# Two blocks of a transformer on one core: who brings 96 of the 128 rows of the last block of expert weights, and when

## The reference, cut to what matters

```
xe = jax.vmap(lambda hb, ib: hb[ib])(h, idx)
hidden = jax.nn.silu(jnp.einsum('becd,edf->becf', xe, w_gate)) * jnp.einsum('becd,edf->becf', xe, w_up)
ye = jnp.einsum('becf,efd->becd', hidden, w_down) * gate[..., None].astype(h.dtype)
return jax.vmap(lambda ib, yb: jnp.zeros((t, d), yb.dtype).at[ib.reshape(-1)].add(yb.reshape(-1, d)))(idx, ye)
```

## Time and profile before

| | us |
|---|---|
| time, median of 3 runs | 1834.66 (1834.52 to 1834.79) |
| time of the profiled execution | 1835.42 |
| its span | 1833.6 |
| TensorE busy (matmul) | 1443.5, 79% of the span |
| VectorE busy | 689.1, 38% |
| ScalarE busy | 527.5, 29% |
| moved by DMA | 542.02 MB, mean 296 GB/s |

### The profile page before, as it was taken

How to read it: one execution, slowest core, us unless ns; L and a number is a source line. 1 busy time by engine, 2 the same in 40 slices (tenths; PEclk the granted TensorE clock), 3 DMA queues, 4 the chain that set the end, 5 groups by cost and what they waited for, 6 DMA issues and landing times.

```text
span 1833.6 us, 24325 instructions
## 1 busy us (share of the span) xinstructions
PE 1443.5 (79%) x10242; PEld 943.9 (51%) x10251; DVE 689.1 (38%) x1169; ACT 527.5 (29%) x879; POOL 120.2 (7%) x147
## 2 busy tenths in 40 slices
PE   7999999999999999999895565665556655556565
PEld 7887888887888889988642111211111111111121
DVE  5676666666666667887620000000000000000000
ACT  6545443654444576566510000000000000000000
POOL 0151000012000011042200000000000000000000
PEclk9999999999999999999998778878777787887878
DMA  9533555543455644434789999999999999999997
GB/s 274 178 122 129 188 188 184 177 144 116 161 193 193 193 142 139 137 97 184 315 350 426 428 428 427 428 428 426 427 428 428 428 428 427 427 428 428 428 427 324
DMA packets 139283, 542.02 MB, mean 296 GB/s; under 512 B 10173, under 2 KB 103570, under 8 KB 114738
## 3 DMA queue, kind: packets, MB, share of 16 engines
q1 hardware_dynamic: 138968, 540.46, 75.0%
q0 software_dynamic: 48, 0.13, 0.0%
q10 hardware_dynamic: 170, 0.04, 0.0%
HBM read 539.56 MB, written 1.05 MB: 295 GB/s over the span
## 4 chain that ended last, share of the span: by engine, by line
PE 46%; DMA 45%; DVE 4%; ACT 2%; issue 1%; POOL 0%; ACTq 0%; SPq 0%; DVEq 0%; POOLq 0%
DMA ew<-in_expert_w_up_dram 15%; DMA ew<-in_expert_w_gate_dram 15%; DMA ew<-in_expert_w_down_dram 14%; PE bank L1310 8%; PE bank L1617 7%; PE bank L1312 7%; PE bank L1311 7%; PE bank L1615 4%; PE bank L1995 3%; DVE wHL L2056 1%; PE bank L2033 1%; PE bank L1614 1%; PE bank L1533 1%; ACT wHL L825 1%; PE bank L1331 1%
## 5 line engine op out<-in xcount | busy, mean ns | idle before, releaser
L1995 PE MATMUL bank<-ew,xeT 128*32 128x512 f32 x2048 | 342.7, 805 | 233.8 <-DMA ew<-in_expert_w_up_dram 127.7
L2056 DVE TENSOR_TENSOR wHL<-ring,wHL 128x2048 fp32r<-128x2048 f32 (+1 forms) x124 | 284.3, 2294 | 103.3 <-ACT wHL L825 102.6
L1995 PEld LDWEIGHTS bank<-ew,xeT 128*32 128x32 f32 x2048 | 65.0, 129 | 492.3 <-DMA ew<-in_expert_w_up_dram 208.3
L825 ACT ACTIVATE wHL<-ring 128x2048 fp32r<-128x2048 f32 (+1 forms) x124 | 236.6, 1908 | 244.8 <-PE bank L1617 132.2
L2033 PE MATMUL bank<-ew,tok 128*32 128x256 f32 x2048 | 158.6, 464 | 104.8 <-DMA ew<-in_expert_w_down_dram 97.2
L1617 PE MATMUL bank<-xHL,wHL 128*128 128x512 f32 x588 | 210.0, 396 | 0.0
L2761 DVE TENSOR_TENSOR tok<-tok,bank 128x512 f32<-128x512 f32 x16 | 11.0, 688 | 524.7 <-PE bank L1995 524.7
L1615 PE MATMUL bank<-xHL,wHL 128*128 128x256 f32 x672 | 174.1, 279 | 0.0
L2033 PEld LDWEIGHTS bank<-ew,tok 128*32 128x32 f32 x2048 | 71.8, 128 | 186.3 <-DMA ew<-in_expert_w_down_dram 119.5
L2766 DVE TENSOR_TENSOR h<-h,bank 128x512 f32<-128x512 f32 x60 | 37.2, 681 | 293.0 <-PE bank L2041 293.0
L1615 PEld LDWEIGHTS bank<-xHL,wHL 128*128 128x128 f32 x672 | 126.6, 188 | 8.2
(11 more groups left out here) (358 smaller groups left out, 2248.9 us busy)
## 6 DMA issues: line engine op xcount, KB each, us to landing
ew<-in_expert_w_gate_dram SPq DMA_DIRECT2D x64, 2048.0 KB, 46.2
ew<-in_expert_w_up_dram SPq DMA_DIRECT2D x64, 2048.0 KB, 46.0
ew<-in_expert_w_down_dram SPq DMA_DIRECT2D x62, 2048.0 KB, 46.7
ring<-in_w_gate_up_dram SPq DMA_DIRECT2D x44, 1024.0 KB, 5.0
ring<-in_w_down_dram SPq DMA_DIRECT2D x22, 1024.0 KB, 4.9
ring<-in_w_in_dram SPq DMA_DIRECT2D x22, 1024.0 KB, 5.3
ring<-in_w_out_dram SPq DMA_DIRECT2D x12, 1024.0 KB, 4.9
ring<-in_w_in_fox_dram SPq DMA_DIRECT2D x10, 1024.0 KB, 9.4
```

Of the source, the lines that this page charges most:

```text
L825: act.activation(split_part(n, 0, 0, w.stop), ring[:, slot(n), w], ACT.Copy).then_inc(w_hi, 1)
L1995: mm = pe.matmul(bank[half][32 * j:32 * j + 32, :], xeT[:, k, CAP * e:CAP * e + CAP], w_[:, m, 512 * j:512 * j + 512], start=(k == 0), sto ...
L2056: op = dve.tensor_tensor(split_part(n, 1, c0, c1 - c0), ring[:, slot(n), c0:c1], split_part(n, 0, c0, c1 - c0).bitcast(F32), ALU.subtract)
```

## The change

SP's three parts of the last unit hold only rows (partitions) 96 to 127: 32 rows instead of 128. Rows 0 to 95 are issued by ScalarE, whole rows of 16 KB, in twelve transfers of 8 rows. ScalarE issues them ahead of its work for the last expert, when unit 181 has been used, the same condition as SP's for its parts. They count on a semaphore of their own (`e_near`), 16 for each, and TensorE waits for all twelve before the first matmul of the last unit. The bytes moved and all the arithmetic stay as they are.

```diff
@@
+        NEAR, NEAR_ROWS = 96, 8
...
-        e_end = x_in[0]
+        e_end, e_near = x_in[0], x_in[1]
...
-                    sp.dma_start(ew[:, eslot(g), c], src[:, c]).then_inc((e_full[eslot(g)], e_rest, e_end)[part], 16)
+                    sp.dma_start(ew[NEAR:P, eslot(g), c], src[NEAR:P, c])\
+                        .then_inc((e_full[eslot(g)], e_rest, e_end)[part], 16)
...
             for e in range(NE):
+                if e == NE - 1:
+                    act.wait_ge(e_used, LAST - ESLOTS + 1)
+                    near = e_down[0, e].rearrange("(u p m) d -> u p (m d)", p=P, m=4)[EU - 9]
+                    for r in range(0, NEAR, NEAR_ROWS):
+                        act.dma_start(ew[r:r + NEAR_ROWS, eslot(LAST), :], near[r:r + NEAR_ROWS, :]).then_inc(e_near, 16)
                 act.wait_ge(e_used, e * EU + 4)
...
                 for j in range(4):
+                    if e * EU + 8 + j == LAST:
+                        pe.wait_ge(e_near, 16 + 16 * (NEAR // NEAR_ROWS))
                     w_ = arrived(8 + j).rearrange("p (m d) -> p m d", m=4)
```

## The result

The changed kernel takes 1861.12 us (median of 6 runs, 1858.04 to 1866.78), the kernel before 1834.59 (6 runs, 1834.14 to 1835.40): a ratio of 1.015 with a 95% interval of 1.0139 to 1.0160, 26.5 us slower. Forecast were 1833.1 us and a range of 1832.4 to 1840.6. The profiled execution has a span of 1859.5 us (time 1861.33).

A forecast was written before the change was run, and what follows sets the result against it. The experts' stage was taken as bound by the DMA weight stream at 428 GB/s. Last bytes 3.5 us sooner, less lost cover of small parts, gave -1.6 us from 1834.66: 1833.1 us, range 1832.4 to 1840.6.

The forecast's parts named there:

- a transfer of 8 rows runs on eight engines: ScalarE's twelve transfers: one row per engine, always the same eight engines, 192 packets more in q10.
- issues of ScalarE: ScalarE's queue: twelve issues at 0.30 to 0.73 us take 3.6 to 8.8 us, ending 1784.0 to 1789.2.
- SiLU: ScalarE's work behind the issues: at 1788.50 before, still starts by 1790; 0.7 us late costs nothing against 21 us.
- the half that is ahead: End of the weight stream: the eight engines given more rows finish early, by about 1818.0; called the weakest step.
- The cost of taking turns: Eight engines serving two queues for some 15 us: taken as nothing, at most 0.6 us a row, 7.2 us.
- The other bound: From instruction packets, 1.2 us for 16 KB against 0.61: up to 0.6 us more per row, twelve times, 7.2 us.
- unit 190's first matmul: TensorE, next-to-last unit: starts at about 1820.9, since ScalarE's twelve rows go ahead of that unit's.
- units 190 and 191 as two whole units: TensorE at the end: 3.8 us for both without a wait, last matmul at 1824.7 against 1826.32 before.
- Rival D: Right half, but turns cost what instruction packets show: unit 190 lands at 1828.05, +5.6 us, 1840.2; chance 0.20.
- rival B: Load shared evenly, six rows to each of 16 engines, ahead of unit 190: +1.9 us, 1836.6; chance 0.10.
- Rival C: The eight engines are the half behind: unit 190 lands at 1828.05, +5.6 us, 1840.2; chance 0.20.
- the gap between the halves: End of the weight stream: eight engines end on average at 1816.9, eight at 1823.3; 6.4 us or 10.4 rows.

The follow-up runs named there:

- 128 rows by columns: Against the changed kernel, ScalarE issues all 128 rows with three quarters of their columns, SP the last quarter: 1836.40 us, ratio 1.0014.
- rows in place: Against the changed kernel, ScalarE issues eight transfers of rows r, r+4, ... r+28, rows 64 to 127 not loaded, SP none of the last unit: 1835.80 us.
- spread rows: Against the changed kernel, each of ScalarE's twelve transfers takes every twelfth row: 1848.84 us; the same transfers issued by SP in its own queue: 1845.17 us.

## Why the prediction was wrong

The forecast was 1.6 us faster and the kernel is 26.5 us slower. Step by step:

| step of the prediction | forecast | measured |
|---|---|---|
| "a transfer of 8 rows runs on eight engines" | 192 packets more in q10 | 192 |
| issues of ScalarE | 3.6 to 8.8 us | 4.39 us |
| SiLU | starts by 1790, no cost | 1792.21, later than said, at no cost |
| "the half that is ahead" | all eight | six of eight |
| **"The cost of taking turns": "I take nothing"**, at most 0.6 us for a row, on eight engines | 0, at most 7.2 us | all 16 engines at half of their rate for 44 us: 22.1 us |
| unit 190's first matmul | 1820.9 | 1848.58 |
| units 190 and 191 as two whole units | 3.8 us | 3.66 us |

**What failed.** The step that failed is "The cost of taking turns", the term for rows beside the stream: taken at nothing, at most 7.2 us on eight engines; it measured 22.1 us on all sixteen. The prediction counted rows for each DMA engine, which was right, and never asked which rows an engine has. It priced the queue and not the rows. The rows of the trace chosen for it, the start of the program, had 0.5 KB rows and 0.04 MB in all on the second queue, and SP's queue alone moved 366 GB/s there, not 428; they could not show what 16 KB rows do to each other. The other bound, 0.6 us more for a row, had nearly the right size for the mean packet (1.23 for 0.62), but was charged only to the twelve rows of eight engines. In truth the rows of the stream itself are slowed as much, on all sixteen engines.

**Rival D** had the right side: a row beside the stream costs something. Its +5.6 us was a fifth of the loss, and its mechanism was wrong, as the kernels with 128 rows by columns and with rows in place show: a second queue costs +2.1 us with all of the turns and none of the collisions. That is **rival B**'s +1.9, which comes from rows ahead of unit 190. **Rival C** is true of two engines of eight.

**How far the sum closes.** The stream loses 22.1 us by the windows. What is left of 26.5 is 4.4, and rival C's price for rows ahead of unit 190 on engines that are behind, 5.6 us, is the nearest figure for it. With the one transfer of 96 rows the stream loses 24 x (1 - 341/428) = 4.9 us and 0.9 just before, of 12.2; with spread rows 24 x (1 - 291/428) = 7.7 and about 2 around it, of 15.2. In both of these TensorE takes 5.3 us for the last two units, for 3.66 in the change, at its lower clock, which is 1.7 us more. What is left is 4.7 and about 4 us. This rest of 4 to 5 us in all three was worked out and not measured by itself.

**The range** ended at 1840.6 because the highest price in it was for eight engines. The lower end was never near.

**What stays open.** Why eight neighbours cost the whole stream half of its rate, including engines whose groups nobody else writes, is open. That every engine was slowed is shown; it was not by waiting for a free place, as SP had issued everything by 1784. That one slow engine holds up the others of its transfer, or that the share counts a packet's waiting as busy, is argued and not shown. Whether the rows meet where they are written or where they are read was not tested. Why spread rows in SP's queue are as slow as neighbours there, why 96 rows over all groups are slow on ScalarE's queue, and every other row not slow at all, would need to be seen engine by engine; the profile gives a mean over 16. And the gap between the halves, 6.4 us, was not closed by any kernel here: the eight engines that a small transfer uses are not the half ahead, and rows given to other engines fall, by the place theory, into groups that are full. None of the twelve kernels beat the kernel before.

## What to carry to other kernels

Where the DMA engines are the bound, count not only how many rows each engine moves but also which rows it moves, and keep the transfers of the stream at 128 partitions unless a run of the very cut shows that it is free; the cut by columns was. A DMA share of 1.00 is not a full rate: read the share and the GB/s together, and work out the time of a packet from them. A price taken from small packets at the program's start said nothing here about full rows beside a saturated stream.

## What the runs showed of the hardware

- Twelve transfers of 8 neighbouring rows of 16 KB beside a stream of 128-row transfers: 213 GB/s for 428 over 44 us, at a DMA share of 1.00.
- Eight transfers of 8 rows to the same eight engines: 0.63 us for a packet when row r + 4i goes to the i-th, 1.05 when the rows are neighbours, and 7.4 us of time between the two kernels.
- One transfer of 96 rows beside the stream: 221 GB/s while it moves, 12.2 us of time.
- Two transfers of 64 neighbouring rows in place of one of 128: landing 6.3 us later, 9.8 us of time; even rows and odd rows: the same landing, and a time that can't be told apart.
- A second queue with 1.5 MB in 128-row form beside the stream: 427 GB/s, no loss.
- A late landing cost more than its lateness in the kernel of two halves: after an idle stretch of 5.43 us TensorE had the 1.2 GHz clock and took 3.64 us for a unit that takes 1.93 at 2.4 GHz.
